# One core, two-layer diffusion backbone: in the first layer's last chunk, a pair of multiply-adds, the gate's context group and the output weights' splits are put in other steps

## What is computed

```python
h = x * (1.0 + sc) + sh                       # modulated latent tokens; hc likewise for the context
q, k, v, z = jnp.split(h @ w_in[l], 4, axis=-1)
...
s_loc = q·k of an 8 x 16 window * scale + bias; s_ctx = q·kc * scale
p = softmax([s_loc, s_ctx])
y = p_loc·v_win + p_ctx·vc                     # 16 heads of 64
...
out = (y * silu(z)) @ w_out[l]                # z: the gate
x_new = layer_norm(ALPHA * x + (1.0 + g) * out, ln_g[l], ln_b[l])
```

## Time and profile before

| | us |
|---|---|
| median of 3 runs | 1802.76 |
| lowest, highest | 1802.66, 1803.04 |
| profiled execution, whole | 1802.79 |
| its span (first to last instruction) | 1801.0 |
| TensorE busy in the span | 1764.9 (98%) |
| VectorE, ScalarE, GpSimd busy | 1264.3, 907.5, 287.7 |

### The profile page before, as it was taken

How to read it: one execution, slowest core, us unless ns; L and a number is a source line. 1 busy time by engine, 2 the same in 40 slices (tenths; PEclk the granted TensorE clock), 3 DMA queues, 4 the chain that set the end, 5 groups by cost and what they waited for, 6 DMA issues and landing times. The chain is left out here.

```text
span 1801.0 us, 30653 instructions
## 1 busy us (share of the span) xinstructions
PE 1764.9 (98%) x10381; PEld 1526.2 (85%) x10381; DVE 1264.3 (70%) x2260; ACT 907.5 (50%) x1624; POOL 287.7 (16%) x251
## 2 busy tenths in 40 slices
PE   7999999999999999989999999999999999999998
PEld 4898989888888888878878988888888888898886
DVE  6677776767676767774978576685848485857658
ACT  2555555565555656570045556464737465554500
POOL 3200000000000000265441010100001010102951
PEclk9999999999999999999999999999999999999999
DMA  9414141413223231334512020202020110202343
GB/s 349 112 52 110 45 110 41 107 51 99 62 81 79 60 101 49 112 97 166 188 71 51 13 61 2 60 12 61 12 50 23 31 41 16 57 12 60 102 156 119
DMA packets 125376, 138.56 MB, mean 77 GB/s; under 512 B 84833, under 2 KB 93185, under 8 KB 125201
## 3 DMA queue, kind: packets, MB, share of 16 engines
q1 hardware_dynamic: 111504, 111.73, 20.5%
q0 software_dynamic: 11088, 16.78, 4.2%
q10 hardware_dynamic: 2736, 9.44, 1.3%
HBM read 106.54 MB, written 17.73 MB: 69 GB/s over the span
## 5 line engine op out<-in xcount | busy, mean ns | idle before, releaser
L525 PE MATMUL acc<-h_hi,w_hi 128*128 128x512 f32 (+1 forms) x1408 | 523.0, 371 | 2.3 <-DVE w_lo L508 1.2
L525 PE MATMUL acc<-h_hi,w_lo 128*128 128x512 f32 (+1 forms) x1408 | 508.5, 361 | 0.0
L525 PE MATMUL acc<-h_lo,w_hi 128*128 128x512 f32 (+1 forms) x1408 | 508.3, 361 | 0.0
L525 PEld LDWEIGHTS acc<-h_hi,w_lo 128*128 128x128 f32 x1408 | 265.6, 189 | 41.3
L525 PEld LDWEIGHTS acc<-h_hi,w_hi 128*128 128x128 f32 x1408 | 266.0, 189 | 39.3 <-DVE h_lo L450 3.4
L525 PEld LDWEIGHTS acc<-h_lo,w_hi 128*128 128x128 f32 x1408 | 266.4, 189 | 33.8
L1664 DVE TENSOR_REDUCE stats<-acc 128x1 f32<-128x1280 f32 x128 | 189.7, 1488 | 38.6 <-PE acc L1771 36.9
L1580 ACT ACTIVATE far_pt<-acc 128x512 f32<-128x512 f32 (+1 forms) x192 | 101.2, 527 | 162.0 <-PE acc L1780 158.7
L1573 ACT ACTIVATE far_prob<-acc,stats 128x1280 f32<-128x1280 f32 x128 | 170.2, 1330 | 24.1 <-DVE stats L1664 22.3
L1771 PE MATMUL acc<-k_dup,q_stack 128*128 128x512 f32 (+1 forms) x768 | 176.8, 367 | 1.8 <-ACT far_prob L1573 0.6
L1793 PE MATMUL acc<-far_v,far_pt 128*128 128x128 f32 x1280 | 172.7, 275 | 0.0
(11 more groups left out here) (209 smaller groups left out, 2920.6 us busy)
## 6 DMA issues: line engine op xcount, KB each, us to landing
w_raw<-in_w_in SPq DMA_DIRECT2D x64, 512.0 KB, 3.3
near_late_slots<-in_w_mod SPq DMA_DIRECT2D x64, 256.0 KB, 2.7
w_raw<-in_w_out SPq DMA_DIRECT2D x16, 512.0 KB, 3.3
w_raw<-y_t POOLq DMA_DIRECT2D x14, 448.0 KB, 5.2
near_values<-near_values POOLq DMA_DIRECT2D x16, 384.0 KB, 4.2
far_v<-far_v_blocks SPq DMA_DIRECT2D x128, 40.0 KB, 2.1
y_t<-y SPq DMA_DIRECT2D x7, 640.0 KB, 3.0
modulation_rows<-in_w_scale SPq DMA_DIRECT2D x8, 512.0 KB, 6.4
```

What stands on the lines that cost most here:

```text
L525: mm = nc.tensor.matmul(m.bank(self.bank_of(j, c), w), wt[:, b % 2, k, :], ht[:, k, t0:t0 + w], start=(k == 0 and i == 0), stop=(k == KT - ...
```

## The change

Three things are moved, all in the last chunk (`last` is True) of the first layer:

- `late.sum` 5 goes from the end of step 3 to the end of step 0, behind the finishing of gate group z1.
- z2's 8 k-tiles go from step 1 (4 in the middle, 4 at the end) to the middles of steps 1 (2), 2 (2) and 3 (4). Its tanh and `gate_silu` go with it, from the end of step 1 to the end of step 3.
- The high parts of the output weights go from steps 2 (k = 0, 1), 3 (k = 2), 4 (k = 3) to steps 3 (k = 0, 1) and 4 (k = 2, 3); k = 4 to 7 stay in steps 5 to 8.

`fill` and `filled` become tables by `last`; the chunks of the loop do what they did.

```diff
-    filled = {step: piece[0:2] for (step, half), piece in fill.items() if piece[3] == KT}
+    fill_of = {False: fill, True: {at: piece for at, piece in fill.items() if not piece[0] and piece[1] != z2}}
+    fill_of[True].update({(1, MIDDLE): (0, z2, 0, 2), (2, MIDDLE): (0, z2, 2, 4), (3, MIDDLE): (0, z2, 4, 8)})
+    filled_of = {last: {step: piece[0:2] for (step, half), piece in fill_of[last].items() if piece[3] == KT} for last in (False, True)}
...
-    OUT_SPLITS = {2: (0, 1), 3: (2,), 4: (3,), 5: (4,), 6: (5,), 7: (6,), 8: (7,)}
+    OUT_SPLITS = {3: (0, 1), 4: (2, 3), 5: (4,), 6: (5,), 7: (6,), 8: (7,)}
...
-                        if step == 3 and last:
+                        if step == 0 and last:
                             late.sum(v, c, 5)
```

More of the change, by code:

```diff
@@ L1155, in take_filled @@
                     def take_filled(step):
-                        if step in filled:
-                            next_chunk, j = filled[step]
+                        if step in filled_of[last]:
+                            next_chunk, j = filled_of[last][step]
                             if not next_chunk:
                                 p.gate_tanh(act, c, j)
-                            elif j < 3 and not last:
+                            elif j < 3:
                                 p.evacuate(act, c + 1, j)
@@ L1295, in chunk @@
                             scale_gate(step // 2 - 1)
-                        if step in filled and not filled[step][0]:
-                            p.gate_silu(v, c, filled[step][1])
+                        if step in filled_of[last] and not filled_of[last][step][0]:
+                            p.gate_silu(v, c, filled_of[last][step][1])
                         if step == 4 and not last:
                             p.split_lo_part(v, nc.vector, c, 5)
-                        if step == 3 and last:
+                        if step == 0 and last:
                             late.sum(v, c, 5)
@@ L1395, in fill_in @@
                             after.part(pe, 0, 1, k0, k1)
-                        if (step, half) not in fill:
+                        if (step, half) not in fill_of[last]:
                             return
-                        next_chunk, j, k0, k1 = fill[step, half]
-                        if next_chunk and last:
-                            return
+                        next_chunk, j, k0, k1 = fill_of[last][step, half]
                         if j == z1 and k0 == 0:
```

## The result

| | before | after |
|---|---|---|
| median, us (8 runs each, same chip) | 1803.54 | 1808.74 |
| lowest, highest | 1802.66, 1804.40 | 1808.36, 1809.85 |
| profiled execution, whole (span) | 1802.79 (1801.0) | 1808.66 (1806.9) |

The ratio is 1.0031, with a 95% interval from 1.0022 to 1.0041: slower, by some 5 us. The prediction was 1806.9 with a range from 1804.5 to 1808.5, so it had the sign right and the size too small; the measured time lies 0.24 us above the range. Of the 1.84 us between 1808.74 and 1806.9, 0.75 is the starting point: the forecast was added to 1802.79, and the kernel before has a median of 1803.54 here. The other 1.05 is the difference, 5.20 instead of 4.15.

What follows compares the result with a forecast made beforehand. TensorE is busy 98% of the span, but in steps 2 to 8 the chain of VectorE and ScalarE sets the beat. Sum: 0.9 - 1.1 + 0.25 + 4.1 = 4.15 on 1802.79, so 1806.9 us, range 1804.5 to 1808.5.

Steps and rivals of the forecast that it cites:

- Sum 5 in step 0: VectorE, behind z1's finishing: the sum delays step 1 by 1.33 us, z2's finishing gives back 0.44, step 2 begins 0.9 later.
- TensorE's gaps in step 1: Sign in the profile after: TensorE idle some 3 us in step 1, where its second z2 piece is gone.
- z2 in steps 2 and 3: TensorE: six matmuls in step 2 (0.7 us) and twelve in step 3 (1.4 us) lie in waits and cost nothing.
- Step 3, 5.96 us: VectorE: step 3 shrinks from 7.06 to 5.96 us, losing sum and high parts, gaining z2's finishing; step 4 begins 0.2 earlier.
- the first wait for w_raw: ScalarE, end of step 4: first of two waits for output weight loads, about 1.9 us.
- High parts 2 and 3, the term that decides: ScalarE, end of step 4: loads wait for GpSimd's low parts behind z2; step 5's first batch 4.35 us later, 4.15 remain.
- The sharing: Load 7 right behind load 3 slows load 3 by 0.65 us, within 0 to 1.3.
- the first rival: Load 3 isn't slowed by load 7 and lands in 3.16 us: +3.5 us, 1806.3; chance 0.20.
- The chain of steps 5 to 9 only shifts: After step 5's late first batch, later steps keep their distances; from step 6 on all rows come 4.15 us later.
- the fifth rival: TensorE's clock falls to 1.2 GHz after idling about 2.2 and 1.6 us in step 5: some 3 us more, 1810; chance 0.05.
- a sign of being wrong: Wrong if the granted clock falls, ScalarE doesn't wait for w_raw at step 4's end, or a later step gives time back.

Runs made afterwards that it cites:

- sum_ahead: Kernel before, with only late sum 5 moved to step 0, ahead of z1's finishing: -0.99 us, ratio 0.9993, stretch 60.79 us against 61.71.
- sum_behind: Kernel before, with only late sum 5 moved to step 0, behind z1's finishing: +0.27 us, ratio 1.0001, stretch 62.14 us against 61.71.
- mended: Change with sum 5 ahead of z1's finishing, GpSimd's low parts 0 and 1 ahead of `split_head` 1, high parts one a step from step 4: -0.82 us against before.
- head_later: Change with GpSimd making low parts 0 and 1 ahead of `split_head` 1 and its wait for z2: +5.50 us against the kernel before, ratio 1.0030.
- busy_twice: Change with unused extra matmuls in TensorE's gaps, seven in step 1, twelve in step 5, real piece ahead of the values: +4.17 us against before, ratio 1.0022.
- splits_spread: Change with the output weights' high parts one a step from step 4 on: +2.79 us against the kernel before, ratio 1.0013.
- load7_later: Change with late load 7 issued behind output weight load 4 instead of load 3: +5.72 us against the kernel before, ratio 1.0029.
- keep_busy: Change with twelve unused matmuls in step 5 and the real piece ahead of the values: +5.12 us against the kernel before, ratio 1.0027.
- sum_back: Change with late sum 5 put back at the end of step 3: +5.57 us against the kernel before, ratio 1.0028.

## Why the prediction was too low

**Sum 5 in step 0: right.** Predicted +0.9 for step 2, measured +0.75. sum_ahead and sum_behind, 1.35 apart in the stretch, show that its position behind z1's finishing costs what the argument said. TensorE's gaps in step 1 were 1.75 and 0.95 us, near the "some 3 us".

**z2 in steps 2 and 3: right.** No wait of TensorE's names it, and mended, with the same dealing, is within 0.3 us of sum_ahead.

**Step 3, 5.96 us: wrong, but hidden.** It took 773.81 - 766.54 = 7.27, 1.31 more, and 1.30 of that is the gating, 1.72 instead of 0.42 us. The prediction took each engine's rows of before by themselves and moved GpSimd's L1913 beside another VectorE instruction without asking what they do to each other. head_later shows the cause: with L1913 elsewhere, 0.41. The 1.3 vanished in the first wait for w_raw, predicted as 1.9 and measured as 1.01: ScalarE came to it 1.3 later, and the load was there 0.4 later.

**High parts 2 and 3, the term that decides: right.** GpSimd's start 770.25 was 770.46 (corrected), its first low part 773.35 was 773.55, ScalarE's second high part 781.9 was 782.15, the first batch 782.9 was 783.11, and the sum of step 5 came +4.34 late, where 4.15 was forecast. That it fits to 0.2 us is in part luck. GpSimd's start was 0.2 late and its low parts took 4.87 instead of 4.71 us, which made load 3's issue 0.35 late; against that the load was read 3.70 us after its issue instead of 3.81, in the slowest case of five. The sharing was mis-sized, 0.65 for a measured 0.1 to 0.4, so the first rival's mechanism, a load 3 that is hardly slowed, was nearly right.

**"The chain of steps 5 to 9 only shifts": wrong, and this is the step that failed.** It was the fifth rival's case, given 0.05: the idle times of step 5 (1.85 and 1.38; the prediction had 2.2 and 1.6) brought the granted clock to 0.50, which the prediction had named as a sign of being wrong. Its size was wrong in the other direction, "some 3 us" for a measured 1.56, since most of step 5's work lay ahead of the gaps and only its last values, step 6's scores and three transposes ran at 1.2 GHz. 4.34 + 1.56 = 5.90 is the measured shift; busy_twice, with the gaps filled, comes to +4.02, near the forecast of 4.15. So the mechanism up to step 5 was right, and the sum put the clock, 1.56 us in the profile and some 1.0 in the medians, at nothing. The evidence that the rows of before gave was that in the last chunk no gap, 1.4 us at most, had moved the clock; longer gaps had no row at all, and that is no ground for 0.05. The same trace also held a fall that no row shows: at 34.2 us of the span the clock went to 0.50 for some 3 us, behind several gaps of 0.68 to 0.83 us in which TensorE waited for loads. The Trainium skill, "TensorE: Matmul & The Clock Gate", part on the clock gate, says that an idle engine goes back to the lower level, which had stood beside the rival; the trace agrees, at 0.50 behind gaps of 1.85 and 1.38 us.

**What stays open.** Whether the clock falls in step 1 differs between executions: same gaps, 1.00 in the profiles of the change and head_later, 0.50 to 0.57 in those of splits_spread, load7_later and keep_busy. The same holds for the place at 34 us. How often it falls in either step, and so how the median divides between the wait and the clock, one profile for each kernel can't say; the mean granted clocks of the other executions (0.995 to 0.999) move with their times, but don't tell the places.

## What to carry to other kernels

Follow a moved piece of work to the last engine that hangs on it (here z2, GpSimd's low parts, SP's loads, ScalarE, VectorE, TensorE), and don't place two loads of a chain ahead of one step's first batch. For every instruction that ends up beside another engine's at a new time, ask whether the two share something. When a forecast opens a gap on the engine whose clock can fall, price the fall as a term with a chance of its own, not as a mishap, and look through the whole trace, not only the part that is changed, for stretches in which the clock had fallen and for the gaps ahead of them.

## What the runs showed of the hardware

- **VectorE and GpSimd hold each other up** when both read two operands from SBUF. Gating: 1.69 to 1.93 us instead of 0.42 beside L1913; the pair of multiply-adds: 3.52 and 5.26 us instead of 1.41 beside L887, which itself took 5.55 and 5.29 instead of 4.71. The gating of the change ended 0.3 us after L1913 did (773.47 and 773.18), the 5.26 of sum_back 0.5 us after the low parts. Where no such pair stood beside L887 it took 4.71, as before, in head_later and mended. Instructions with one operand in PSUM were not held up: L569, `gate<-gate,acc`, took 0.41 beside L887. The Trainium skill, "GPSIMD Engine Reference", section "Specifications", names such a contention for VectorE instructions with two SBUF inputs; the size is from these runs.
- **The clock fell after two gaps of 1.85 and 1.38 us** with 0.5 us of work between, stood at 0.50 for some 3.3 us and cost 1.56. In some executions it fell after 1.75 and 0.95 us, and in some, at the start of the program, after a row of gaps of 0.68 to 0.83 us; in others with the same gaps it didn't. In a gap of 6.63 us (sum_back) it fell within the gap and stood at 0.50 for some 10 us, 4.3 of them still in the gap.
- **A load of 512 KB** with 256 KB issued 0.4 us behind it took 3.37 to 3.70 us from issue to its reader's start (five kernels), 3.28 without (load7_later).
